# Opening of a hybrid decoder step: order of the first loads, the way the first norm is applied, and how eight gate columns are multiplied

## What is computed

```python
h = rmsnorm(x, norm_mix)                 # x * rsqrt(mean(x^2) + eps) * w
p = h @ w_in                             # 1024 x 6152: q, f, i, g, qkv (conv), a_b, b_b, z, gates
# a_b and b_b: 4 + 4 columns; g = -exp(a_log) * softplus(a_b + dt_bias), beta = sigmoid(b_b)
# HGRN2 mixer from q, f, i; Gated DeltaNet mixer from conv(qkv), beta, g; both recurrent in chunks
x = x + mixers(p)
x = x + moe(rmsnorm(x, norm_ffn))        # top 4 of 32 experts, clamped SwiGLU
y = rmsnorm(x, norm_final)
```

## Time and profile before

| | |
|---|---|
| time, median of 3 runs | 1393.54 us (1391.24 to 1399.49) |
| the profiled execution | 1391.47 us, its span 1389.7 us |
| TensorE matmuls, busy | 1322.1 us (95% of the span) |
| VectorE, busy | 472.8 us (34%) |
| ScalarE, busy | 191.5 us (14%) |
| GpSimd, busy | 51.0 us (4%) |
| DMA | 450.94 MB, mean 324 GB/s |

### The profile page before, as it was taken

The page is one execution under the profiler, slowest core; times in us unless marked ns, Lnnn a source line. Parts: engine busy times, 40 slices in busy tenths (PEclk is TensorE's granted clock), DMA queues, the critical chain, the costliest instruction groups (busy, mean ns, idle before and its releaser), DMA issues.

```text
span 1389.7 us, 18885 instructions
## 1 busy us (share of the span) xinstructions
PE 1322.1 (95%) x7049; PEld 573.6 (41%) x7049; DVE 472.8 (34%) x980; ACT 191.5 (14%) x327; POOL 51.0 (4%) x139
## 2 busy tenths in 40 slices
PE   3999898998989999999999999999999999999995
PEld 3777675766443333333333333333333333333321
DVE  2044457444444332223332222332222332222333
ACT  2113531221311000000000000000001000000002
POOL 2000210200100000000000000000000000000000
PEclk9999899999979999999999999999999999999997
DMA  9144120824919999999999999999999999999892
GB/s 286 63 146 157 63 71 19 280 83 120 368 62 375 419 417 417 416 418 418 419 418 416 417 418 419 419 419 417 417 417 419 419 418 418 417 416 418 349 409 104
DMA packets 103985, 450.94 MB, mean 324 GB/s; under 512 B 11697, under 2 KB 20987, under 8 KB 71078
## 3 DMA queue, kind: packets, MB, share of 16 engines
q1 hardware_dynamic: 96552, 442.91, 79.5%
q10 hardware_dynamic: 7398, 7.56, 2.1%
HBM read 444.27 MB, written 6.26 MB: 324 GB/s over the span
## 4 chain that ended last, share of the span: by engine, by line
PE 67%; DVE 1%; issue 0%; ACT 0%; DVEq 0%
PE ps L914 31%; PE ps L939 17%; PE ps L892 7%; PE ps L872 6%; PE ps L886 2%; PE ps L900 1%; PE ps L880 1%; PE ps L909 1%; PE ps L932 1%; DVE x_tok L1683 0%; DVE x_tok L1657 0%; ACT proj L1174 0%; ACT proj L1170 0%; DVE proj L1639 0%; DVE proj L1642 0%
## 5 line engine op out<-in xcount | busy, mean ns | idle before, releaser
L914 PE MATMUL ps<-ring,proj 128*64 128x512 f32 x2048 | 466.3, 598 | 0.0
L939 PE MATMUL ps<-ring,proj 128*64 128x512 f32 x1024 | 247.4, 606 | 0.7 <-ACT proj L1170 0.7
L914 PEld LDWEIGHTS ps<-ring,proj 128*64 128x64 f32 x2048 | 141.3, 137 | 256.7 <-issue 248.4
L1657 DVE TENSOR_TENSOR x_tok<-x_tok,ps 96x512 f32<-96x512 f32 x192 | 122.8, 679 | 113.5 <-PE ps L892 113.5
L1632 DVE TENSOR_SCALAR proj<-ps 128x512 f32<-128x512 f32 x32 | 22.1, 692 | 404.0 <-PE ps L914 404.0
L939 PEld LDWEIGHTS ps<-ring,proj 128*64 128x64 f32 x1024 | 65.7, 137 | 152.6 <-issue 150.3
L892 PE MATMUL ps<-proj 64*96 64x512 f32 x384 | 106.8, 633 | 3.6 <-DVE x_tok L1657 2.8
L552 PE MATMUL ps<-feat,ring 128*128 128x288 f32 x384 | 100.0, 415 | 0.0
L542 PE MATMUL ps<-feat,ring 128*128 128x288 f32 x384 | 95.2, 412 | 0.0
L872 PE MATMUL ps<-proj 96*64 96x512 f32 x384 | 90.5, 607 | 0.0
L542 PEld LDWEIGHTS ps<-feat,ring 128*128 128x128 f32 x384 | 74.2, 194 | 20.6
(11 more groups left out here) (334 smaller groups left out, 880.3 us busy)
## 6 DMA issues: line engine op xcount, KB each, us to landing
ring<-in_w_gu SPq DMA_DIRECT2D x256, 1024.0 KB, 16.7
ring<-in_w_down SPq DMA_DIRECT2D x128, 1024.0 KB, 15.8
ring<-in_w_in SPq DMA_DIRECT2D x12, 2048.0 KB, 8.1
out<-states SPq DMA_DIRECT2D x1, 2048.0 KB, 8.7
ring<-in_w_oa SPq DMA_DIRECT2D x1, 2048.0 KB, 7.7
ring<-in_w_ob SPq DMA_DIRECT2D x1, 2048.0 KB, 10.6
ring<-in_w_out SPq DMA_DIRECT2D x1, 2048.0 KB, 8.0
out<-states ACTq DMA_DIRECT2D x1, 2048.0 KB, 10.0
```

Source lines behind the costliest of these rows:

```text
L914: last = mm(bank(j // 2)[64 * (j % 2):64 * (j % 2) + 64, :], xgT[:, k % 4, k // 4, :], ring[:, k, 512 * j:512 * j + 512], start=False, sto ...
L939: last = mm(bank(4)[64 * j:64 * j + 64, :], hidT[:, k % 4, 64 * (k // 4):64 * (k // 4) + 64], ring[:, KT + k // 2, n:n + 512], start=False ...
L1657: tt(x, x, bank(5 + j)[0:TP, :], ALU.add).then_inc(sg["comb_taken"], 1)
```

## The change

- The SyncE queue starts with x tiles 1 and 2, then x tile 0, the first chunk of w_in, the gate columns, `state_conv`, two more chunks, and then `state_hgrn` and the router weights. The six parameter loads move to the head of the ScalarE queue. `w_ab`, with 32 columns for each feature tile of which 24 are zeros, lies in the work area.
- The x tiles are handled in the order 1, 2, 0. Each has its own square root and reciprocal; ScalarE makes one square root on `epsb` ahead of them. VectorE writes a diagonal matrix of the reciprocals (`diag_x`, 96 x 96), and TensorE computes x^T times this diagonal as plain matmuls in place of the transposes of a scaled x.
- The gate columns: 8 matmuls of a 128 x 32 stationary piece by 128 x 288 of `feat`; feature tiles 2g and 2g+1 accumulate into output partitions 32g to 32g+31, VectorE copies the 128 x 288 result (`ab_rows`), and three small matmuls with `diag` add the four groups and transpose. This stands after projection tile 2, and the small matmuls after tile 3.
- The 12 transposes of `buf_rows` follow behind these, and the rolled loop over the first 24 tiles is written out.
- VectorE makes the router scaling after the g operations; tile 28 moves ahead of the wait for `l2_root`.

```diff
     NEARLY = 24
+    X_ORDER = (1, 2, 0)
...
-        w_ab = sb("w_ab", [128, KT, 2 * H])
...
+        w_ab = wk(4736, KT * C).rearrange("p (k c) -> p k c", k=KT)
+        ab_rows = wk(5040, T)
+        diag_x = wk(5328, NI * TP, TP).rearrange("p (i t) -> p i t", i=NI)
...
-            sp.dma_start(prm_rows[0:KT, :], norm_mix.rearrange("l (k p) -> (l k) p", p=128)).then_inc(sg["prm_in"], 16)
...
-            sp.dma_start(prm_rows[66:74, :], norm_ffn.rearrange("l (k p) -> (l k) p", p=128)).then_inc(sg["prm_in"], 16)
             sp.dma_start(x_tok[:, 1, :], x_prompt[0, 64:160, :]).then_inc(sg["x_in1"], 16)
...
-            sp.dma_start(buf_rows, state_conv[0].rearrange("b j d -> (b j) d")).then_inc(sg["buf_in"], 16)
-            sp.dma_start(w_ab[:], w_in[0, :, AB0:AB0 + 2 * H].rearrange("(k p) n -> p k n", p=128)).then_inc(sg["ab_in"], 16)
...
             for n in range(NCHUNK - 1):
                 win_load(n)
+                if n == 0:
+                    sp.dma_start(w_ab[:, :, 0:2 * H], w_in[0, :, AB0:AB0 + 2 * H].rearrange("(k p) n -> p k n", p=128)) \
+                        .then_inc(sg["ab_in"], 16)
+                    sp.dma_start(buf_rows, state_conv[0].rearrange("b j d -> (b j) d")).then_inc(sg["buf_in"], 16)
+                if n == 2:
+                    sp.dma_start(states[:], state_hgrn[0].rearrange("b h k v -> k (b h) v")).then_inc(sg["stA_in"], 16)
+                    sp.dma_start(w_rt[:], w_router[0].rearrange("(k p) n -> p k n", p=128)).then_inc(sg["route_in"], 16)
...
-            L(gp.memset(epsb[:], RMS_EPS))
+            gp.sem_inc(sg["consts"], 1)
+            L(gp.memset(w_ab[:, :, 2 * H:C], 0.0))
...
             pe.wait_ge(sg["consts"], 1)
             pe.wait_ge(sg["prm_in"], 96)
-            pe.wait_ge(sg["buf_in"], 16)
-            tr(bank(0)[:, 0:74], prm_rows[0:74, :], ident[0:74, 0:74])
-            for f in range(FC):
-                last = tr(bank(1)[:, 24 * f:24 * f + 24], buf_rows[:, 128 * f:128 * f + 128], ident[0:24, 0:24])
-            last.then_inc(mark["prm_turned"][0], 1)
-
-            for i in range(NI):
-                pe.wait_ge(sg["x_normed"], i + 1)
+            tr(bank(0)[:, 0:74], prm_rows[0:74, :], ident[0:74, 0:74]).then_inc(mark["prm_turned"][0], 1)
+
+            for p, i in enumerate(X_ORDER):
+                pe.wait_ge(sg["x_normed"], p + 1)
                 for k in range(KT):
-                    last = tr(bank(2 + 2 * i + k // 4)[:, TP * (k % 4):TP * (k % 4) + TP], xh[:, i, 128 * k:128 * k + 128],
-                              ident[0:TP, 0:TP])
+                    last = mm(bank(2 + 2 * i + k // 4)[:, TP * (k % 4):TP * (k % 4) + TP], x_tok[:, i, 128 * k:128 * k + 128],
+                              diag_x[:, i, :], start=True, stop=True)
                 last.then_inc(sg["x_turned"], 1)
 
             pe.wait_ge(sg["feat_ready"], 2 * NI)
             pe.wait_ge(*mark["prm_ready"])
+
+            def early_tile(n):
+                if n % 4 == 0:
+                    pe.wait_ge(sg[f"win_in{n // 4 % NRING}"], 16 * (n // 4 // NRING + 1))
+                pe.wait_ge(sg["bank_free"], n + 1)
+                for k in range(KT):
+                    last = mm(bank(4 + n % 4)[:, 0:T], win_buf[n // 4 % NRING][:, k, 128 * (n % 4):128 * (n % 4) + 128],
+                              feat[:, k, :], start=k == 0, stop=k == KT - 1)
+                last.then_inc(sg["ptile_done"], 1)
+
+            for n in range(3):
+                early_tile(n)
+            pe.wait_ge(sg["consts"], 2)
             pe.wait_ge(sg["ab_in"], 16)
+            for a in range(2):
+                for g in range(4):
+                    last = mm(bank(0)[C * g:C * g + C, 0:T], w_ab[:, 2 * g + a, :], feat[:, 2 * g + a, :],
+                              start=a == 0, stop=a == 1)
+            last.then_inc(mark["ab_rows_done"][0], 1)
+            early_tile(3)
+            pe.wait_ge(*mark["ab_copied"])
             for i in range(NI):
-                for k in range(KT):
-                    last = mm(bank(0)[0:TP, 8 * i:8 * i + 8], feat[:, k, TP * i:TP * i + TP], w_ab[:, k, :],
-                              start=k == 0, stop=k == KT - 1)
+                last = mm(bank(1)[0:TP, 8 * i:8 * i + 8], ab_rows[:, TP * i:TP * i + TP], diag[:, 0:2 * H],
+                          start=True, stop=True)
             last.then_inc(mark["ab_done"][0], 1)
-
-            with pe.Fori(0, NEARLY // (4 * NRING)) as it:
-                for j in range(NRING):
-                    pe.wait_ge(sg[f"win_in{j}"], 16 * (it + 1))
-                    for m in range(4):
-                        pe.wait_ge(sg["bank_free"], 12 * it + (4 * j + m) + 1)
-                        for k in range(KT):
-                            last = mm(bank(4 + m)[:, 0:T], win_buf[j][:, k, 128 * m:128 * m + 128], feat[:, k, :],
-                                      start=k == 0, stop=k == KT - 1)
-                        last.then_inc(sg["ptile_done"], 1)
+            pe.wait_ge(sg["buf_in"], 16)
+            for f in range(FC):
+                last = tr(bank(2)[:, 24 * f:24 * f + 24], buf_rows[:, 128 * f:128 * f + 128], ident[0:24, 0:24])
+            last.then_inc(mark["buf_turned"][0], 1)
+            for n in range(4, NEARLY):
+                early_tile(n)
...
-            pe.wait_ge(*mark["ab_taken"])
+            pe.wait_ge(*mark["buf_taken"])
...
+            project(28, 29)
             pe.wait_ge(sg["l2_root"], 2)
             pe.wait_ge(*mark["g_ready"])
...
-            project(28, 30)
+            project(29, 30)
...
+            act.dma_start(prm_rows[0:KT, :], norm_mix.rearrange("l (k p) -> (l k) p", p=128)).then_inc(sg["prm_in"], 16)
...
+            act.dma_start(prm_rows[66:74, :], norm_ffn.rearrange("l (k p) -> (l k) p", p=128)).then_inc(sg["prm_in"], 16)
             act.dma_start(alb, a_log.to_broadcast([TP, H])).then_inc(sg["par_in"], 16)
             act.dma_start(dtb, dt_bias.to_broadcast([TP, H])).then_inc(sg["par_in"], 16)
-            act.dma_start(states[:], state_hgrn[0].rearrange("b h k v -> k (b h) v")).then_inc(sg["stA_in"], 16)
-            act.dma_start(w_rt[:], w_router[0].rearrange("(k p) n -> p k n", p=128)).then_inc(sg["route_in"], 16)
+            act.wait_ge(*mark["eps_ready"])
+            L(f(smx[:, 0, 0:1], epsb[:, 0:1], ACT.Sqrt))
+            for p, i in enumerate(X_ORDER):
+                act.wait_ge(sg[f"x_in{i}"], 16 if i else 48)
+                L(f(xh[:, i, :], x_tok[:, i, :], ACT.Square, accum_out=ss[:, i:i + 1]))
+                L.tell(f(rstd[:, i:i + 1], ss[:, i:i + 1], ACT.Sqrt, scale=1.0 / D, bias=epsb[0:TP, 0:1]), "x_summed", p + 1)
             act.dma_start(conv_sample[0, :, 0:CW - 2, :], state_conv[0, :, 1:CW - 1, :]).then_inc(sg["conv_stored"], 16)
-            for i, n in enumerate((48, 16, 16)):
-                act.wait_ge(sg[f"x_in{i}"], n)
-                L(f(xh[:, i, :], x_tok[:, i, :], ACT.Square, accum_out=ss[:, i:i + 1]))
-            act.wait_ge(sg["consts"], 1)
-            L.tell(f(rstd, ss, ACT.Sqrt, scale=1.0 / D, bias=epsb[0:TP, 0:1]), "x_summed")
             act.wait_ge(sg["par_in"], 32)
             L(f(alb, alb, ACT.Exp))
             act.wait_ge(*mark["lb_diff"])
...
+            L.tell(v.memset(epsb[:], RMS_EPS), "eps_ready")
             dve.wait_ge(*mark["prm_turned"])
-            L(v.tensor_copy(prmT, bank(0)[:, 0:74]))
-            L.tell(v.tensor_copy(bufT.rearrange("p f b j -> p (f b j)"), bank(1)[:, 0:288]), "prm_ready")
-
-            dve.wait_ge(sg["route_in"], 16)
-            L.tell(tt(w_rt[:], w_rt[:], prmT[:, 66:74].rearrange("p (k o) -> p k o", o=1).to_broadcast([128, KT, NE]), ALU.mult),
-                   "w_rt_ready")
+            L.tell(v.tensor_copy(prmT, bank(0)[:, 0:74]), "prm_ready")
+            dve.wait_ge(sg["consts"], 1)
+            for p, i in enumerate(X_ORDER):
+                dve.wait_ge(sg["x_summed"], p + 1)
+                L(v.reciprocal(rstd[:, i:i + 1], rstd[:, i:i + 1]))
+                L.tell(ts(diag_x[:, i, :], ident[0:TP, 0:TP], rstd[:, i:i + 1], None, ALU.mult), "x_normed", p + 1)
+            for p, i in enumerate(X_ORDER):
+                dve.wait_ge(sg["x_turned"], p + 1)
+                for j in range(2):
+                    src = bank(2 + 2 * i + j)[:, 0:4 * TP].rearrange("p (k t) -> p k t", k=4)
+                    w = prmT[:, 4 * j:4 * j + 4].rearrange("p (k o) -> p k o", o=1).to_broadcast([128, 4, TP])
+                    L.tell(tt(feat[:, 4 * j:4 * j + 4, TP * i:TP * i + TP], src, w, ALU.mult), "feat_ready", 2 * p + j + 1)
+            dve.sem_inc(sg["bank_free"], 4)
+            dve.wait_ge(sg["consts"], 2)
             L(tt(lbt, prmT[:, 8:12], prmT[:, 12:16], ALU.max))
             L(tt(omlb, prmT[:, 12:16], lbt, ALU.subtract))
...
-            dve.wait_ge(sg["x_summed"], 1)
-            L(v.reciprocal(rstd, rstd))
-            for i in range(NI):
-                L.tell(ts(xh[:, i, :], x_tok[:, i, :], rstd[:, i:i + 1], None, ALU.mult), "x_normed", i + 1)
...
```

(44 more changed lines are left out.)

4 lines of the change are left out of this document (removed).

## The result

| | median | runs | ratio to before, 95% interval |
|---|---|---|---|
| before, beside it | 1395.77 us | 5 | 1 |
| changed | 1384.99 us | 5 (1383.74 to 1385.34) | 0.9918, 0.9901 to 0.9934 |

The change makes the kernel 10.8 us faster (about 8.5 us against the 1393.54 us of the first three runs of before), where 15.5 us was forecast; 1384.99 us lies inside the range of 1372 to 1388 and 7 us above the predicted time. The profiled execution took 1385.16 us, its span is 1383.4 us, so the two traces differ by only 6.3 us. That they differ by less than the medians is a finding of its own (runs e0 and e8).

A forecast was written before the change was run, and what follows sets the result against it. TensorE work, mostly expert matmuls, was taken to bound the kernel. Gains of 7.2 (opening), 3.9 (tile 28) and 4.4 us (clock staying up) made 15.5, from 1393.5 to 1378.0 us; range 1372 to 1388.

The forecast's parts named there:

- A: Main forecast: opening 7.2, tile 28 3.9, clock staying up after it 4.4; 15.5 us gained, 1378.0 us; chance 0.40.
- the wait: Before the fifth projection tile: TensorE idles 5.2 us because ScalarE's first tile copy is queued behind the g chain.
- well off 45 us: Stated sign of being wrong: the fifth projection tile starts well off 45 us.
- the opening's sum: Terms from the start up to the fifth projection tile: 46.6 us against 53.8, a gain of 7.2 us.
- the diagonal product's price: Opening: 24 transposes become 48 fp32 matmul records at 0.21 us, 10.1 us at the lower clock level.
- D: Rival: the diagonal product lifts the clock early, 5 us more gain than A, 1373 us; chance 0.07.
- F: Rival: the diagonal product costs four times the transposes, 6.3 us more, some 1384 to 1389 us; chance 0.06.
- gate columns: Opening: 7.85 us of gate matmuls leave the path; 16 records on separate quarters of the array take 1.1 us.
- the first tile: Opening: the first projection tile starts at 18.8 us, against 36.1 in the kernel before.
- rival C: Opening: x or the parameters land up to 5 us late, 1383 to 1388 us; chance 0.13.
- the slow clock: Fifth projection tile: starts at the lower clock level after the idle, costing 2.2 us, bounds 0 and twice that.
- B: Rival: the clock falls in the 3.0 us left idle after tile 28; gain 11.1 us, 1382.4 us; chance 0.30.

The follow-up runs named there:

- e0: The kernel before, unchanged, run again for a second trace; 1395.81 us, ratio 1.0018.
- e8: The kernel before with the state_hgrn and router-weight loads moved to SyncE's queue behind three w_in chunks, router scaling behind the g operations; 1387.56 us, ratio 0.9953.
- e1: The changed kernel with ScalarE's copies of projection tiles 0 to 3 ahead of the g chain; 1378.14 us, ratio 0.9891.
- e5: The changed kernel with ten unused matmuls put into TensorE's wait before the fifth tile; 1381.43 us, ratio 0.9907.
- e3: The changed kernel with x scaled by VectorE and turned by true transposes in place of the diagonal product; 1378.31 us, ratio 0.9899.
- e9: The kernel before, unchanged, run for a third trace; 1392.43 us (one run).
- e2: The changed kernel with tile 28 put back behind the conv rows; 1390.54 us, ratio 0.9967.
- a0: The changed kernel, unchanged, run again for a second trace; 1385.39 us, ratio 0.9928.
- e7: The changed kernel with both copies of tiles 0 to 3 first and true transposes; 1371.89 and 1371.50 us, ratios 0.9851 and 0.9840.

## Why the prediction was right or wrong

The time lies in the range, and that is in part luck: of A's three gains (7.2 + 3.9 + 4.4) the last never came and the first was 3.2. The traces show 5.5 us of what the sum was about; the other half of the measured 10.8 us has causes that weren't in it.

**Right: the wait.** That the g chain stands ahead of the first copy, and so stops TensorE before the fifth tile, was forecast at 5.2 us, with the tile's start at 44.4; it took 5.58 and the tile started at 47.27. e1 and e5 confirm cause and double price. By its own sign, a fifth tile "well off 45 us", the opening's sum was off by 2.3 to 2.9 us, for the reasons below.

**Right: the diagonal product's price.** 48 x 0.21 = 10.1 us from L590's records (7 of the 31 were the shorter ones of L591); 10.56 measured. D (upper clock) and F (four times the transposes) didn't occur. The Trainium skill, "TensorE: Matmul & The Clock Gate", section Terms, gives a factor of four for fp32 transpose mode; here it is 10.56 against 4.10 us for the same 24 blocks, 2.6, so the measurement decides. The rule of the Trainium skill pointed the right way all the same, which my text did not draw out: against true transposes the edit is a loss, 5.8 us of the opening in e3.

**Right: gate columns.** 1.1 us forecast, 36.25 - 35.14 = 1.11 measured, 0.29 of what 16 records take in a row (3.88).

**Wrong: the first tile, 20.7 us against 18.8.** The step that failed is "the parameter rows ... by the early end they are there at 5". The last landed at 7.43, 4.6 us after its issue at 2.78, while x and w_in streamed; I had taken the 2.1 us of a load on an idle queue. The root of x1 was done at 6.96 us and VectorE could only take it at 8.17, so this is 1.2 of the 1.9 us. The rest is ScalarE's start (5.49 in place of 5.1) and the product (10.56 in place of 10.1). x itself was there when ScalarE first asked. It is rival C in its small form.

**Wrong in size: the slow clock.** I took 2.2 us after the wait, from tile 0 of before. Counted as there, against 3.88, the tile took 3.4 too long; against e5 it is 3.0 to 3.1, since 0.4 us from the last matmul to the copy is in either. The first three tiles too took 14.4 us where 13.8 was in the sum. Their slow records in the changed kernel:

```profile
L534 PE MATMUL ps<-feat,ring x11: 604/687/818, 20.7 to 25.6; 128*128 128x288 f32 x11
```

From 26.1 us on the records are at full rate, 5.4 us after the first tile's start, where the first trace of before needed 3.8. But this isn't a trait of either kernel: e9, the kernel before, also has 11 slow records, e1 and e2 have 7, and the three tiles took 13.4 to 14.4 us in the traces with the changed opening. A bound of 0 to 4.4 was right to state.

**Wrong: A in place of B.** "The clock stays up after tile 28" had 0.40 against 0.30 and fell in all eight traces that have the edit. The sum for B was 11.1 us. First tile 1.9, slow start 0.6, wait 0.4 and slow fifth tile 1.2 are 4.1 late, which leaves 7.0. A further 1.5 is lost behind the broadcasts, which I had not charged: conv rows 0.4 and tile 29 1.1 (5.04 us to the next step against 3.93), both at the lower clock. That leaves 5.5, and the traces show 5.5 at the product behind it.

**Not foreseen: what the trace of before left out.** The sum was made against one execution in which the router weights came in time. In e0 they did not and the whole opening was 3.4 us later. So "I take gains from it and put times on the median" was too simple: the change also removes this delay, and that can be in the medians (10.8 us in one comparison, 10.1 in the other) and not in the pair of traces (6.3). How much of the 4 us between them it is, and how much the clock's dips, isn't shown. I had put the late squares down to x sharing the DMA engines; e8 shows that the two loads were in the way also by their issue, on the engine that had to square x. Of e8's gain I can't say how much is the router wait; no run separates the three.

**The rest of the way.** Between the broadcasts and the experts the pair of traces drifts, from 5.5 us at 172 down to 1.0 at 357 to 400 and up to 6.3 at the end, with the same work in the same order. One step down, of 1.1 us, is a wait that was 1.11 us for VectorE before and is longer now:

```profile
349.06 5.34 PE L822 MATMUL ps<-ring,feat 128*96 128x512 f32 x8 [2.25 <-DMA states<-in_w_out]
```

It is the second half of w_out. Its load is issued 4.2 us earlier than before (336.98 against 341.19) but takes 12.0 us to land in place of 10.3; why is open. a0, e1 and e2 wait for it too, in e3 and e7 VectorE ends the wait after 1.1 us. The other steps are slow-clock stretches in other places, 1.7 us of them in the very matmuls of this line (5.34 us against 3.67). In the last expert block L954 takes 7.09 us in the changed kernel, in both of its traces, and 9.38 in before (L939), 9.28 in e1, 8.78 in e3 and e7. Those are 2.3 us that no part of the change was meant to give. That a dip's place follows from where the program's gaps fall is argued from the repeats (after and a0 agree to 0.2 us all the way), not shown by an experiment.

## What to carry to other kernels

Starting an engine earlier is worth only what is left at the first resource that is freed in someone else's program order: before moving work ahead, look up what the engine that frees the buffers has queued in front of the release. Keep bulk loads and what waits for them off the engine and queue that the first computation needs; here that alone gave 6.6 us, and the whole rebuilt opening without its tile 28 gave 5.0 (the intervals overlap). And put no arithmetic into a transpose to save an elementwise pass that is hidden beside it.
